# The down-projection of a decoder trunk's second feed-forward layer by seven block products in place of eight, with block sums made on GpSimd and VectorE

## The reference, cut to what matters

```python
D_MODEL = 1024
D_FF = 2816

def swiglu(x, w_in, w_out):
    gate, up = jnp.split(x @ w_in, 2, axis=-1)
    return (jax.nn.silu(gate) * up) @ w_out

def decoder_layer(...):
    ...
    h = h + rmsnorm(merged @ p['w_o'], p['mix_post'])
    y = h + 0.5 * rmsnorm(swiglu(rmsnorm(h, p['ffn2_pre']), p['ffn2_w_in'], p['ffn2_w_out']), p['ffn2_post'])
    return y, k_rows, va, new_conv, new_S
```

## Time and profile before

| what | value |
|---|---|
| median of three runs | 3400.17 us |
| the profiled execution, from its first to its last instruction | 3400.1 us |
| TensorE (PE) busy in it | 97% |
| VectorE (DVE), ScalarE (ACT), GpSimd (POOL) busy | 55%, 43%, 21% |
| first and last matmul of the changed stage | 3119.1 and 3388.8 us |
| TensorE clock granted in the last 300 us | 1.00, at the very end 0.96 |

### The profile page before, as it was taken

One profiled execution on the slowest core, in us unless ns is written; L12 is line 12 of the kernel. 1 busy time (PEld: TensorE's weight loads), 2 busy tenths in 40 slices (PEclk: granted clock), 3 DMA queues, 4 the chain that ended last, 5 costly groups with the idle time before them and its releaser, 6 DMA issues. The chain is left out here.

```text
span 3400.1 us, 70872 instructions
## 1 busy us (share of the span) xinstructions
PE 3305.8 (97%) x28190; PEld 3137.6 (92%) x28190; DVE 1871.2 (55%) x3334; ACT 1456.3 (43%) x3056; POOL 700.0 (21%) x651
## 2 busy tenths in 40 slices
PE   7999999998999999999999999999999899999999
PEld 7999999997888888877899999998999899999998
DVE  6655565764555555554455555554441855556555
ACT  5222234555555455443344444444323722223444
POOL 3323310112222222100022222222001332221000
PEclk9999999999999999999999999999999999999999
DMA  4222237742222222379511122224532322224664
GB/s 167 76 79 79 87 109 230 221 135 81 70 70 70 71 70 70 109 254 369 188 47 56 58 59 59 59 59 136 165 88 70 123 86 76 76 76 151 200 207 132
DMA packets 353606, 390.03 MB, mean 115 GB/s; under 512 B 22792, under 2 KB 259416, under 8 KB 353134
## 3 DMA queue, kind: packets, MB, share of 16 engines
...
## 5 line engine op out<-in xcount | busy, mean ns | idle before, releaser
L673 PE MATMUL ps<-p_hi,w_hi 128*128 128x352 f32 x912 | 305.6, 335 | 1.8 <-PEq L123 1.4
L673 PE MATMUL ps<-p_hi,w_lo 128*128 128x352 f32 x912 | 294.5, 323 | 0.0
L673 PE MATMUL ps<-p_lo,w_hi 128*128 128x352 f32 x912 | 294.0, 322 | 0.0
L2062 PE MATMUL ps<-p_hi,w_hi 128*128 128x352 f32 x840 | 291.0, 346 | 2.7 <-PEq L123 1.4
L2062 PE MATMUL ps<-p_hi,w_lo 128*128 128x352 f32 x840 | 277.2, 330 | 0.0
L2062 PE MATMUL ps<-p_lo,w_hi 128*128 128x352 f32 x840 | 277.2, 330 | 0.0
L673 PEld LDWEIGHTS ps<-p_hi,w_hi 128*128 128x128 f32 x912 | 173.1, 190 | 4.2 <-issue 2.7
L2897 PE MATMUL ps<-op_hid_hi,w_hi 128*128 128x384 f32 (+1 forms) x528 | 171.5, 325 | 3.7 <-DVE w_lo L2572 2.0
L673 PEld LDWEIGHTS ps<-p_lo,w_hi 128*128 128x128 f32 x912 | 173.2, 190 | 0.0
L2897 PE MATMUL ps<-f_hid_hi,w_hi 128*128 128x352 f32 x528 | 171.5, 325 | 1.6 <-DVE w_lo L2572 1.6
L673 PEld LDWEIGHTS ps<-p_hi,w_lo 128*128 128x128 f32 x912 | 172.2, 189 | 0.0
(11 more groups left out here) (707 smaller groups left out, 10374.4 us busy)
## 6 DMA issues: line engine op xcount, KB each, us to landing
w_raw<-in_ffn_w_out_dram SPq DMA_DIRECT2D x136, 256.0 KB, 3.4
...
sa_v<-in_cache_v_dram SPq DMA_DIRECT2D x120, 256.0 KB, 6.7
...
sa_k<-in_cache_k_dram SPq DMA_DIRECT2D x72, 256.0 KB, 5.5
f_s<-in_ffn_w_out_dram SPq DMA_DIRECT2D x64, 256.0 KB, 3.5
pair_s<-in_ffn_w_out_dram SPq DMA_DIRECT2D x64, 256.0 KB, 3.2
d_hid<-f_gb SPq DMA_DIRECT2D x44, 264.0 KB, 2.1
```

Of the source, the lines that this page charges most:

```text
L673: mm = nc.tensor.matmul(m.ps[:, bank, 0:CH], a[:, k, w], b[:, f, cols(c)], start=(f == 0 and i == 0), stop=(f == KT - 1 and i == 2))
L2062: mm = nc.tensor.matmul(m.ps[:, (k + c) % 2, 0:CH], a[:, k, f * P:(f + 1) * P], x[:, f, cols(c)], start=(j == 0), stop=(j == len(terms) - 1))
```

## The change: what it does

The first two chunks (768 tokens) are taken together. The product of the weight matrix (2 x 2 blocks: halves of the hidden rows by halves of the outputs) with the activations (2 x 2 blocks: 11 hidden tiles by 384 tokens, called quads) is made by Strassen's scheme. It has seven products of 11 steps each, in place of eight. The third product is the one of two sums, the fifth one of those with a plain activation block. What this adds:

- Five of the seven products take a sum or difference of two weight blocks. Both tiles are loaded (132 loads in the seven products, in place of 88 in four passes), and GpSimd adds them in place (`w_sum`), 55 additions of 128x512.
- Five take a sum of two activation blocks: in three pieces of 4, 3 and 4 hidden tiles (`x_sum`). In the first product VectorE makes all three; in the others VectorE makes the first and third (128x1536), GpSimd the second (128x1152).
- Casts and subtractions of the activations go by the same three pieces (`x_high`, `x_low`), once for each product.
- The four quads stay in SBUF and are loaded in one transfer each (`load_quad`, 11 x 128 rows of 1,536 bytes, 2.16 MB). The first sum has its own early loads (`load_first_parts`), the third piece of it behind the first quad in SyncE's queue.
- Each product's banks are copied or added into one or two blocks of `acc_chunk`, which is now twice as large (`read_act`, `read_dve`).
- The last chunk (288 tokens) keeps its two passes, but its low parts are made by GpSimd (`rest_low`).
- Squares, scaling, residual and transposes of chunk 0 come in products 6 and 7, those of chunk 1 in the first pass of the last chunk.

```diff
--- before.py
+++ after.py
...
+    KH = FT // 2
+    W3 = 3 * P
+    WL = T - 2 * W3
+    GROUPS = ((0, 4), (4, 7), (7, KH))
+    SOURCES = (((1, 1),), ((0, 1), (1, 1)), ((0, 0), (1, 1)), ((1, 0), (1, 1)), ((0, 0), (1, 0)), ((0, 0),), ((0, 1), (0, 0)))
+    MINUS = (3, 6)
+    NQ = 7 * KH
+    RAWS = [(KH * p + k, n) for p in range(7) for k in range(KH) for n in range(len(SOURCES[p]))] + [(v, 0) for v in range(NQ, NQ + 2 * FT)]
+    RAW_OF = {v: r for r, (v, n) in enumerate(RAWS) if n == 0}
+    SUM_OF = {v: i + 1 for i, v in enumerate(v for v, n in RAWS if n == 1)}
...
+    def load_raw(sp, r):
+        v, n = RAWS[r]
+        if r < 4:
+            sp.wait_ge(e.s_made, 4 * (FT - 3))
+            sp.wait_ge(e.lo_done, 4 + 7 * (FT - 4) + 6)
+        elif r < 8:
+            sp.wait_ge(e.lo_done, 4 + N1)
+        elif RAWS[r - 8][1] == 1:
+            sp.wait_ge(e.w_sum, SUM_OF[RAWS[r - 8][0]])
+        else:
+            sp.wait_ge(e.out_lo, RAWS[r - 8][0] + 1)
+        if v < NQ:
+            p, k = divmod(v, KH)
+            a, half = SOURCES[p][n]
+            k += KH * a
+        else:
+            half, k = divmod(v - NQ, FT)
+        sp.dma_start(unit_raw(r), wout[:, k, half * 512:half * 512 + 512]).then_inc(e.out_full[r % 8], 16)
...
+    def load_first_parts(sp, g):
+        lo, hi = GROUPS[g]
+        if g == 0:
+            sp.wait_ge(e.up_mm, 12 + N1 - 6)
+        else:
+            sp.wait_ge(e.hid_lo, part_count(0, g - 1))
+        sp.wait_ge(e.h_out[0], 16 * (KH + hi))
+        for a in range(2):
+            sp.dma_start(first_part(a, g), d_hid[KH * (1 - a) + lo:KH * (1 - a) + hi, :, 0:W3].rearrange("k p n -> p k n")).then_inc(e.first_in[g], 16)
+
+    def load_quad(sp, a, b):
+        if (a, b) in ((0, 0), (1, 1)):
+            sp.wait_ge(e.up_mm, 12 + N1)
+        else:
+            sp.wait_ge(e.hid_lo, part_count(0, 2))
+        if b == 1:
+            for s in range(2):
+                sp.wait_ge(e.h_out[s], 16 * FT)
+        sp.dma_start(((B11, B12), (B21, B22))[a][b], d_hid[KH * a:KH * a + KH, :, W3 * b:W3 * b + W3].rearrange("k p n -> p k n")).then_inc(e.quad_in[a][b], 16)
...
+        elif p == 2:
+            quad_there(eng, 0, 0)
+            quad_there(eng, 1, 1)
+            if g == 1:
+                eng.wait_ge(e.gate_done, 6 + 2 * (FT - 2))
+                eng.wait_ge(e.up_done, 6 + 2 * (FT - 2))
+            elif g == 0:
+                for s in range(2):
+                    eng.wait_ge(e.h_out[s], 16 * FT)
+            else:
+                eng.wait_ge(e.hid_lo, part_count(2, 0))
+            x, y, op = B11[:, part, :], B22[:, part, :], ALU.add
+        elif p == 3:
...
+            act.wait_ge(e.up_mm, 12 + N1 - 7 + (2, 3, 4, 6)[(GROUPS[g][1] * W3 - 1) // (HALF * HT)])
+        elif p >= 2:
+            act.wait_ge(e.out_mm, KH * (p - 1))
+        nc.scalar.copy(x_slot(hid_hi, p, g), x_value(p, g)).then_inc(e.hid_hi, 1)
...
+    def x_low(dve, p, g):
+        dve.wait_ge(e.hid_hi, part_count(p, g))
+        nc.vector.tensor_tensor(x_slot(hid_lo, p, g), x_value(p, g), x_slot(hid_hi, p, g).bitcast(F32), ALU.subtract).then_inc(e.hid_lo, 1)
+
+    def w_sum(pool, v):
+        r = RAW_OF[v]
+        raw_there(pool, r)
+        raw_there(pool, r + 1)
+        op = ALU.subtract if v // KH in MINUS else ALU.add
+        nc.gpsimd.tensor_tensor(unit_raw(r), unit_raw(r), unit_raw(r + 1), op).then_inc(e.w_sum, 1)
...
+    def w_high(act, v):
+        if v in SUM_OF:
+            act.wait_ge(e.w_sum, SUM_OF[v])
+        else:
+            raw_there(act, RAW_OF[v])
+        if v < 4:
+            act.wait_ge(e.up_mm, 12 + N1 - 10 + v + 1)
+        else:
+            act.wait_ge(e.out_mm, used(v - 4))
+        nc.scalar.copy(unit_slot(v, False), unit_raw(RAW_OF[v])).then_inc(e.out_hi, 1)
+
+    def w_low(dve, v):
+        dve.wait_ge(e.out_hi, v + 1)
+        nc.vector.tensor_tensor(unit_slot(v, True), unit_raw(RAW_OF[v]), unit_slot(v, False).bitcast(F32), ALU.subtract).then_inc(e.out_lo, 1)
...
+    def rest_low(pool, n):
+        pool.wait_ge(e.rest_hi, n + 1)
+        nc.gpsimd.tensor_tensor(rest_tile(hid_lo, n), staged(2, n % 4)[:, 0:WL], rest_tile(hid_hi, n).bitcast(F32), ALU.subtract).then_inc(e.rest_lo, 1)
...
+    def add_block(q, i, j):
+        for half in range(2):
+            y = block_of(i, j, half)
+            if q == 1:
+                nc.vector.wait_ge(e.read_act, READ_ACT[0] + half + 1)
+            nc.vector.tensor_tensor(y, pass_bank(q, half), y, ALU.add).then_inc(e.read_dve, 1)
...
+        load_first_parts(sp, 0)
+        for r in range(4, 8):
+            load_raw(sp, r)
+        load_first_parts(sp, 1)
+        store_h(sp, FT - 1, 0)
+        load_quad(sp, 0, 0)
+        store_h(sp, FT - 1, 1)
...
+        for v in range(NQ):
+            p, k = divmod(v, KH)
+            raws(v + 6 if p else v + 8)
+            if v == 1:
+                load_first_parts(sp, 2)
+            elif v == 5:
+                load_quad(sp, 1, 1)
+            elif v == 13:
+                load_quad(sp, 1, 0)
+            elif v == 30:
+                load_quad(sp, 0, 1)
+            elif v == 62:
+                for n in range(4):
+                    load_rest(sp, n)
...
+    def quad_vector(dve, during):
+        for v in range(NQ):
+            p, k = divmod(v, KH)
+            w_low(dve, v + 3)
+            if p == 0:
+                if k == 0:
+                    x_low(dve, 0, 1)
+                elif k == 4:
+                    x_sum(dve, nc.vector, 0, 2, e.x_sum)
+                elif k == 5:
+                    x_low(dve, 0, 2)
+                elif k in (7, 9, 10):
+                    x_low(dve, 1, {7: 0, 9: 1, 10: 2}[k])
+            else:
+                summed = p + 1 in X_SUM_POOL
+                if k == 0:
+                    read_dve(dve, p - 1, False)
+                elif k == 1 and summed:
+                    x_sum(dve, nc.vector, p + 1, 0, e.x_sum)
+                elif k == 2:
+                    read_dve(dve, p - 1, True)
+                elif k == 3 and p < 6:
+                    x_low(dve, p + 1, 0)
+                elif k == 4 and summed:
+                    x_sum(dve, nc.vector, p + 1, 2, e.x_sum)
+                elif k == 5 and p < 6:
+                    x_low(dve, p + 1, 1)
+                elif k == 7 and p < 6:
+                    x_low(dve, p + 1, 2)
...
+    def quad_gpsimd(pool, during):
+        for p in (1, 2, 3, 4):
+            for k in range(KH):
+                w_sum(pool, KH * p + k)
+                if k == 3 and p + 1 in X_SUM_POOL:
+                    x_sum(pool, nc.gpsimd, p + 1, 1, e.x_sum_pool)
+            during(p)
+        x_sum(pool, nc.gpsimd, 6, 1, e.x_sum_pool)
+        during(5)
+        for k in range(KH):
+            w_sum(pool, KH * 6 + k)
+            if k >= 6:
+                rest_low(pool, k - 6)
+        sum_pool(pool, 1, 1, 4)
+        for n in range(5, 11):
+            rest_low(pool, n)
+        sum_pool(pool, 1, 4, 6)
+        for n in range(11, 13):
+            rest_low(pool, n)
+        sum_pool(pool, 1, 6, 8)
+        for n in range(13, FT):
+            rest_low(pool, n)
...
+    def quad_tensor(pe, during, bank_free):
+        for p in range(7):
+            for k in range(KH):
+                v = KH * p + k
+                during(p, k)
+                pe.wait_ge(e.out_lo, v + 1)
+                for g in range(3):
+                    if k == GROUPS[g][0]:
+                        pe.wait_ge(e.hid_lo, part_count(p, g))
+                x = KH * (p % 2) + k
...
+                    for n, (low_part, y) in enumerate(((False, hid_hi), (False, hid_lo), (True, hid_hi))):
+                        mm = nc.tensor.matmul(m.ps[:, 4 * (p % 2) + o, 0:W3], unit_slot(v, low_part)[:, o * P:(o + 1) * P], y[:, x, :],
+                                              start=(k == 0 and n == 0), stop=(k == KH - 1 and n == 2))
+                mm.then_inc(e.out_mm, 1)
...
+                if h == 5 and k == 6:
+                    pe.wait_ge(e.read_act, 8)
+                    pe.wait_ge(e.read_dve, e.READ_DVE[4])
+                    e.sum_y(pe, 0, 3)
+                if h == 6 and k in (7, 8, 9):
+                    turn(k - 7)
+                if h == 7 and k in (7, 9, 11):
                     turn_residual((k - 7) // 2)
...
+                pairs = {(5, 9): (0, 0), (5, 10): (0, 1), (6, 1): (0, 2), (6, 3): (0, 3), (7, 10): (1, 0), (7, 11): (1, 1), (7, 12): (1, 2), (7, 13): (1, 3)}
+                sums_of = {(6, 4): (0, 0), (6, 5): (0, 1), (7, 14): (1, 0), (7, 15): (1, 1)}
...
-            m.acc_chunk = sb("acc_chunk", [P, KT, 3 * P], to=early)
+            m.acc_chunk = sb("acc_chunk", [P, 2, KT, 3 * P], to=early)
```

More of the change, by code:

```diff
@@ L2836, in gpsimd @@
                 t_low_pool(pool)
+        if quads:
+            quad_gpsimd(pool, during)
     def product(pe, t, i):
@@ L2974, in copy_out, with sum_pool @@
             nc.vector.tensor_copy(result(j)[1], result(j)[0]).then_inc(e.y_copied, 1)
-    def sum_pool(pool, c):
```

(3 more changed lines are left out.)

445 lines of the change are left out of this document (370 added, 75 removed).

## The result

Four runs of each kernel: 3438.22 us median after, 3401.74 before. The ratio is 1.0117, 95% interval 1.0099 to 1.0134: slower, by 36.5 us. The prediction was 3431, the range 3408 to 3453.

The account below looks back on a forecast made before the run. TensorE bounds the kernel before; after the change, VectorE and GpSimd take turns at a shared SBUF port. Terms -22.95 + 10.1 + 22.3 + 4 + 1 + 10 + 3 + 4 = +31.5 on 3400.1: 3431 us, range 3408 to 3453.

Parts of the forecast that it names:

- The rival without turns: Products 2 to 5: wide VectorE pieces don't take turns with GpSimd, or turns fall into idle time; 3391 us, 15%.
- The rival with the queue as a second bound: Loads in SyncE's queue add stalls to the port's, +4 us for each quad in products 2 and 3; 3441 us, 18%.
- (g): First pass of the last chunk: port work of 42.2 us exceeds matmuls and transposes; +3 us (-1 to 7).
- the DMA share of the first two products: Sign in the profile after: DMA share near 1 in products 1 and 2.
- 0.7 us in each step: Sign in products 2, 3 and 5: TensorE idle some 0.7 us a step, put down to VectorE's low parts.
- (a): TensorE: seven products of 132 matmuls replace four passes of 264, 132 matmuls less; -22.95 us.
- (b): First product, step 8: TensorE waits for the third piece of activations; +10.1 us (+3 to +13).
- (h): TensorE's clock falls after the long waits in the first and seventh products; +2 us each, +4 (0 to 8).
- (c): Products 2, 3 and 5: 30.4 us of port turns against TensorE's 22.95; +7.4 us each, +22.3.
- (d): Product 4: port +1.2 us, and a weight slot's way of 7.5 us against 8.34; +4 us (1 to 8).
- (e): Product 6, plain weights: the port serves 25 us, some of it ahead for the seventh; +1 us (0 to 4).
- (f): Product 7: port work of 33 us, transposes at steps 8 to 10 wait for residual sums; +10 us (4 to 15).

Follow-up runs that it names:

- experiments 2 and 5: Against the changed kernel: 2, second weight-sum loads cut to 8 of 512 columns, 3434.3 us; 5, quads loaded in 11 slices each, alone 3438.1 us.
- short sums: Changed kernel with GpSimd's 55 weight sums made over 8 of 512 columns, all loads, casts and low parts kept: 3408.1 us.
- quads in slices: Changed kernel with each quad loaded in 11 slices between the weight tiles: 3438.1 us alone, 3405.4 us together with weight sums over 8 columns.
- experiment 7: Kernel before, with GpSimd additions of 128x512 put into 17 steps of its first pass: 3403.0 us with one a step, 3406.8 us with two.

## Why the prediction was right, step by step

The direction and the main cause hold. The rival without turns (3391) fell to the wide piece of 2.83 us. The rival with the queue as a second bound (3441) is not wholly out, and its number lies nearer to the median than mine: experiments 2 and 5 show that freeing the queue alone gives nothing, but its stall behind a quad is in product 4, and (g) reads like the queue too. Two signs that I had named did not come: the DMA share of the first two products was 0.88 and 0.68 and not near 1, and TensorE's idle time came mostly in a few waits of 1.7 to 4.2 us and not as 0.7 us in each step. By the steps, against the stage's +37.4:

- **(a), -22.95.** Right: 924 matmuls, steps of 2.08 us wherever nothing waits.
- **(b), +10.1.** Product 1 has 13.5 us over 22.95. The wait is 10.96 us (step 7 takes 13.04), the two steps behind it take 3.98 and 2.76, another 2.6 us of (h). Against the 1.9 us that the first pass loses before, +11.6, where (b) with its share of (h) said 12.1. The order that I gave is in VectorE's list:

```profile
3134.99 1.76 DVE L2721 TENSOR_TENSOR plain<-plain 128x1536 f32<-128x1536 f32 x1 [8.50 <-DMA plain<-d_hid]
3138.81 1.47 DVE L2769 TENSOR_TENSOR w_lo<-w_raw,w_hi 128x512 fp32r<-128x512 f32 x1 [2.06 <-ACT w_hi L2765]
3140.20 1.75 DVE L2741 TENSOR_TENSOR op_hid_lo<-plain,op_hid_hi 128x1536 fp32r<-128x1536 f32 x1
```

- **(c), +22.3.** 30.9, 29.4 and 31.1 us: +22.6. The port's 30.4 us a product, put together from rows of before, is their mean, and that is in part luck. I read the 1.75 us of a pair as the sum of its two parts alone, but 0.62 + 1.29 is 1.91: a part of GpSimd's time lies outside the port. Measured, an addition holds it for 1.08 us, not 1.14, and the GpSimd sum of 1152 (2.67 us alone) for 2.49, not 2.8: a VectorE piece of 1536 beside it takes 4.24 us for 1.75. With these the port's sum is 11 x 1.69 + 4.85 + 3.5 + 2.5 = 29.4 us. That is product 3; products 2 and 5 are 1.5 and 1.7 us longer. With short sums products 2 and 5 keep 4.2 and 2.7 us over TensorE's pace, so 15.8 us of the 22.6 go with the weight sums. With the quads in slices as well, products 2, 3 and 5 keep 1.9, 1.9 and 0.
- **(d), +4.** Mis-sized: +8.0. The mechanism was the right one, a slot's way with 0.8 us to spare, but I put the quads in products 2 and 3. The fourth stands in the queue just ahead of product 4's tiles, and a tile of it comes after 9.34 us in the chain of waits:

```profile
3213.36 9.34 DMA w_raw<-in_ffn_w_out_dram
```

GpSimd waits 6.19 us for it, step 4 of the product takes 6.48 and step 5 3.74. In slices the product takes 26.7 us, with short sums 24.5: each of the two takes away half or more of the 8 us, so the late tile costs this much only beside the port's turns.
- **(e), +1.** Right: +0.8.
- **(f), +10, and (h), +2.** Product 7 has 14.4 us over its pace, 3.2 of them the transposes that the third pass had before: +11.3 for 12. With short sums 7.1 of them go (30.3 us). TensorE waits 8.2 us for the second of VectorE's residual sums, which take 2.81 us each beside GpSimd:

```profile
3315.95 2.81 DVE L4497 TENSOR_TENSOR acc_chunk<-acc_chunk,plain 128x1536 f32<-128x1536 f32 x1
...
3319.89 2.81 DVE L4497 TENSOR_TENSOR acc_chunk<-acc_chunk,plain 128x1536 f32<-128x1536 f32 x1
```

Ahead of this stands a part that I had not counted: in the chain a weight tile comes after 7.48 us (from 3305.43 us on), issued behind the residual of 1.5 MB, and VectorE sits idle for 1.84 us before its low part.

- **(g), +3.** Mis-sized, and the waits point to another cause than mine: the rest of the kernel is 6.9 us longer (98.5 for 91.6), 6.5 of it in the first pass of the last chunk, and TensorE's waits there are not put down to low parts but to ScalarE:

```profile
PE ps L4664 <- ACT plain L4357: 4.4, 2, 3.7
```

ScalarE stands in its own list behind the casts of weight tiles that come late; in the chain one of them takes 7.48 us, with the residual (1.5 MB) and three rows of output ahead of it. That it is the queue is read from the trace; no run isolates it, and none takes GpSimd's low parts out of this chunk. Moving the residual's transposes by four steps did not mend it: 100.4 us for the rest, 100.5 without the move.
- **(h), the clock.** The wait of some 11 us is followed by steps of 3.98 and 2.76 us: the granted clock is 0.50, the level of 1.2 GHz, from 3133.9 to 3147.5 us, which is what 0.81 in product 1's row means. Waits of up to 0.7 us cost nothing, as said (1.00 in experiment 7). But products 2 to 5 have waits between the two, for which I had no term. Behind one wait in each (3.3, 2.1, 4.2 and 1.9 us) the clock is at 0.50 for 3.4 us, which gives their 0.94 and 0.95. The steps there take 3.62 us, 2.73 and 3.11, 3.74, and 3.50 in place of 2.08 and are part of (c) and (d); three other waits of 1.7 to 2.1 us had no such stretch behind them.

Sum of the misses: (d) +4.0, (g) +3.9, the others -2.0, together 5.9: 31.5 + 5.9 = 37.4.
